# Starting the input projection inside the first norm: three weight tiles, first token group

## What is computed

```python
h = _rms(x, P['norm_mix_pre'])
proj = jnp.einsum('btd,dc->btc', h, P['w_in'])
hq, hf, hi, hg, rw, sq, sk, sv, gq, gk, gv, ga, gg = _split(proj, IN_WIDTHS)
```

## Time and profile before

| | us |
|---|---|
| median of 3 runs | 2010.35 (2009.53 to 2010.56) |
| span of the profiled execution | 2008.4 |
| TensorE busy | 1819.3 (91%) |
| VectorE busy | 821.1 (41%) |
| ScalarE busy | 614.2 (31%) |
| GpSimd busy | 396.8 (20%) |

### The profile page before, as it was taken

One profiled execution on the slowest core, in us unless ns is written; L12 is line 12 of the kernel. 1 busy time (PEld: TensorE's weight loads), 2 busy tenths in 40 slices (PEclk: granted clock), 3 DMA queues, 4 the chain that ended last, 5 costly groups with the idle time before them and its releaser, 6 DMA issues.

```text
span 2008.4 us, 33890 instructions
## 1 busy us (share of the span) xinstructions
PE 1819.3 (91%) x13839; PEld 1519.3 (76%) x13839; DVE 821.1 (41%) x1320; ACT 614.2 (31%) x1421; POOL 396.8 (20%) x606
## 2 busy tenths in 40 slices
PE   4999999999775798788887996999999999999996
PEld 4999999844454666388873445999999999999995
DVE  7111111166337764734321454344444444433336
ACT  3111111266355554523321222222222222222223
POOL 6400021288335454320010001000000000000004
PEclk9999999999887755689978997999999999999998
DMA  5211131200461111000004101111111111121102
GB/s 150 59 42 34 42 95 56 72 26 1 125 179 41 32 27 29 12 2 2 2 1 156 34 26 53 42 42 42 42 51 54 42 42 42 43 58 45 42 21 89
DMA packets 103829, 100.07 MB, mean 50 GB/s; under 512 B 15522, under 2 KB 89906, under 8 KB 103714
## 3 DMA queue, kind: packets, MB, share of 16 engines
q1 hardware_dynamic: 91266, 81.15, 13.8%
q0 software_dynamic: 6720, 17.11, 2.9%
q10 hardware_dynamic: 5728, 0.19, 0.2%
HBM read 85.78 MB, written 12.65 MB: 49 GB/s over the span
## 4 chain that ended last, share of the span: by engine, by line
PE 51%; DVE 4%; ACT 1%; DMA 1%; issue 1%; POOLq 0%; POOL 0%; SPq 0%; DVEq 0%
PE ps L416 12%; PE ps L418 12%; PE ps L417 12%; PE ps L2422 6%; PE ps L2063 1%; PE ps L2084 1%; PE ps L2080 1%; PE ps L1987 1%; DVE arena L2596 1%; DMA arena<-in_w_out 1%; PE ps L2515 1%; PE ps L2514 1%; PE ps L2136 0%; DVE arena L2173 0%; PE ps L2134 0%
## 5 line engine op out<-in xcount | busy, mean ns | idle before, releaser
L416 PE MATMUL ps<-h_split,w_split 128*128 128x384 f32 (+1 forms) x768 | 251.1, 327 | 3.4 <-DVE w_split L2577 3.4
L418 PE MATMUL ps<-h_split,w_split 128*128 128x384 f32 (+1 forms) x768 | 250.9, 327 | 0.0
L417 PE MATMUL ps<-h_split,w_split 128*128 128x384 f32 (+1 forms) x768 | 250.8, 327 | 0.0
L2607 DVE TENSOR_TENSOR arena<-arena,ps 128x1024 f32<-128x1024 f32 x144 | 175.6, 1220 | 148.7 <-PE ps L418 139.8
L418 PE MATMUL ps<-w_split,u_split 128*128 128x512 f32 x512 | 199.4, 389 | 0.0
L417 PE MATMUL ps<-w_split,u_split 128*128 128x512 f32 x512 | 199.3, 389 | 0.0
L416 PE MATMUL ps<-w_split,u_split 128*128 128x512 f32 x512 | 199.2, 389 | 0.0
L2637 POOL TENSOR_TENSOR arena<-arena 128x1024 f32<-128x1024 f32 (+1 forms) x9 | 22.3, 2482 | 760.1 <-DVE arena L2596 760.1
L2585 DVE TENSOR_TENSOR u_split<-above_u_split,u_split 128x384 fp32r<-128x384 f32 (+1 forms) x96 | 49.4, 515 | 295.9 <-ACT above_u_split L2558 295.8
L2537 ACT ACTIVATE w_split<-below_w_split 128x1024 fp32r<-128x1024 f32 x64 | 64.1, 1048 | 325.0 <-PE ps L418 307.5
L416 PEld LDWEIGHTS ps<-h_split,w_split 128*128 128x128 f32 x768 | 144.7, 188 | 4.2 <-issue 3.6
(11 more groups left out here) (389 smaller groups left out, 3622.5 us busy)
## 6 DMA issues: line engine op xcount, KB each, us to landing
below_w_split<-in_w_up SPq DMA_DIRECT2D x32, 512.0 KB, 5.0
below_w_split<-in_w_down SPq DMA_DIRECT2D x32, 512.0 KB, 4.0
w_raw<-in_w_in SPq DMA_DIRECT2D x27, 512.0 KB, 4.0
arena<-in_x_prompt SPq DMA_DIRECT2D x16, 512.0 KB, 3.7
arena<-in_cache_sb_k SPq DMA_DIRECT2D x64, 128.0 KB, 2.8
arena<-in_cache_sb_v POOLq DMA_DIRECT2D x64, 128.0 KB, 2.9
nat_scratch<-nat_stage POOLq DMA_DIRECT2D x32, 128.0 KB, 2.0
arena<-nat_scratch SPq DMA_DIRECT2D x16, 256.0 KB, 2.8
```

The source lines that it names most:

```text
L416: pe.matmul(out, w_hi, x_hi, start=first, stop=False)
L417: pe.matmul(out, w_hi, x_lo, start=False, stop=False)
L418: return pe.matmul(out, w_lo, x_hi, start=False, stop=last)
L2607: dve.tensor_tensor(y, y, p, ALU.add).then_inc(S("dn_out"), 1)
```

## The change

Nine jobs change their place. Units 0 to 2 run with token group 0 first (jobs 0 to 2), then with group 1 (3 to 5), then with group 2 (6 to 8); the 45 others keep the order of before. Jobs 0 to 2 are cut in half (12 products each) and issued inside the norm, half a job behind the transposes of each of tiles 3 to 8. In front of each of the three jobs TensorE waits for the unit's split and for `hT` 6, the first three tiles of h.

For this SP loads weight tiles 0, 1 and 2 behind tiles 2, 4 and 6, and VectorE splits them behind the scaling and the eviction in its turns 2, 4 and 6. The six banks of the projection are now 4, 5, 6, 7, 3, 0 in that order, the shift transposes go to bank 2, and jobs 4 and 5 wait until the norm has read banks 3 and 0. Job 3 waits for `hT` 12, job 6 for `hT` 18. ScalarE's wait for all of h moves behind its first six evictions. The later units' loads and splits are as before, and the slot and bank bookkeeping follows the new order.

```diff
+EARLY = 3
-    return ([(name, "T", a, tg) for name, a, _ in T_UNITS for tg in range(3)]
+    early = [T_UNITS[u][:2] + (tg,) for tg in range(3) for u in range(EARLY)]
+    late = [(name, a, tg) for name, a, _ in T_UNITS[EARLY:] for tg in range(3)]
+    return ([(name, "T", a, tg) for name, a, tg in early + late]
...
-    PBANKS = 6
+    P_BANKS = (4, 5, 6, 7, 3, 0)
+    PBANKS = len(P_BANKS)
...
                 sp.dma_start(xin[0:rows(i), i % 3, :], x_rows(i)).then_inc(S(f"x_in{i % 3}"), 16)
+                if i in (2, 4, 6):
+                    load_w_in(sp, i // 2 - 1)
...
                 if i >= 1:
                     evac(i - 1)
+                if i in (2, 4, 6):
+                    split_w_in(dve, i // 2 - 1)
...
                     ins.then_inc(S("xT"), 1)
+                if i >= 3:
+                    n, k0 = (i - 3) // 2, KD // 2 * ((i - 3) % 2)
+                    if k0 == 0:
+                        pe.wait_ge(S("w1_split"), n + 1)
+                        pe.wait_ge(S("hT"), 6)
+                    project_T(pe, n, k0, k0 + KD // 2)
 
             pe.wait_ge(S("params"), 16 * N_PAR_DMA)
+            pe.wait_ge(S("h_tmp"), 2 * NT - 3)
             for ct in range(RWT):
-                ins = pe.transpose(ps[:, 6, ct * NB:(ct + 1) * NB], shift_in[0:NB, ct * P:(ct + 1) * P],
+                ins = pe.transpose(ps[:, 2, ct * NB:(ct + 1) * NB], shift_in[0:NB, ct * P:(ct + 1) * P],
...
+        def project_T(pe, n, k0, k1):
+
+            name, _, a, tg = JOBS[n]
+            u = [unit[:2] for unit in T_UNITS].index((name, a))
+            cw, (t0, tw) = T_UNITS[u][2], EG[tg]
+            w_hi, w_lo = (w1[:, y, w_slot(u), :, 0:cw] for y in range(2))
+            for k in range(k0, k1):
+                ins = three(pe, ps[0:cw, P_BANKS[n % PBANKS], 0:tw], w_hi[:, k, :], w_lo[:, k, :],
+                            h_hi[:, k, t0:t0 + tw], h_lo[:, k, t0:t0 + tw], k == 0, k == KD - 1)
+            if k1 == KD:
+                ins.then_inc(S("proj_ps"), 1)
 
         def project_tensor(pe):
-            pe.wait_ge(S("hT"), 2 * NT)
...
+            for n in range(EARLY, NTJ):
+                name, _, a, tg = JOBS[n]
+                if n == EARLY:
+                    pe.wait_ge(S("hT"), 12)
+                if n in (4, 5):
+                    pe.wait_ge(S("h_tmp"), 2 * NT - 2 if n == 4 else 2 * NT - 1)
+                if n == 2 * EARLY:
+                    pe.wait_ge(S("hT"), 2 * NT)
+                if n >= 3 * EARLY and tg == 0:
+                    pe.wait_ge(S("w1_split"), [unit[:2] for unit in T_UNITS].index((name, a)) + 1)
+                if n >= PBANKS:
+                    pe.wait_ge(S("proj_out"), n - PBANKS + 1)
+                project_T(pe, n, 0, KD)
...
         def project_act(act):
-            act.wait_ge(S("hT"), 2 * NT)
-            act.wait_ge(S("shiftT"), 1)
             for n, (name, kind, a, tg) in enumerate(JOBS):
+                if n == 2 * EARLY:
+                    act.wait_ge(S("hT"), 2 * NT)
+                    act.wait_ge(S("shiftT"), 1)
```

More of the change, by code:

```diff
@@ L429, in w_slot_free @@
             v = before[-1]
-            return 3 * (v + 1) if v < len(T_UNITS) else NTJ + NT * ((v - len(T_UNITS)) // 2 + 2)
-        def project_sync(sp):
[L433 to L439, removed]
@@ L441, in project_tensor @@
-        def project_tensor(pe):
-            pe.wait_ge(S("hT"), 2 * NT)
[L443 to L454, removed]
+            if v >= len(T_UNITS):
+                return NTJ + NT * ((v - len(T_UNITS)) // 2 + 2)
@@ new lines, in w_slot_free, with load_w_in, split_w_in @@
+            return JOBS.index((T_UNITS[v][0], "T", T_UNITS[v][1], 2)) + 1
+        def load_w_in(sp, u):
+            name, a, cw = W_UNITS[u]
+            c0 = COL[name] + a * P
+            sp.dma_start(w1_raw[:, u % RSLOTS, 0:KD * cw].rearrange("p (k c) -> p k c", k=KD),
+                         A["w_in"][0].rearrange("(k p) c -> p k c", p=P)[:, :, c0:c0 + cw])\
+                .then_inc(S(f"w_in{u % RSLOTS}"), 16)
+        def split_w_in(dve, u):
+            name, a, cw = W_UNITS[u]
+            raw = w1_raw[:, u % RSLOTS, 0:KD * cw].rearrange("p (k c) -> p k c", k=KD)
+            w_hi, w_lo = (w1[:, y, w_slot(u), :, 0:cw] for y in range(2))
+            dve.wait_ge(S(f"w_in{u % RSLOTS}"), 16 * (u // RSLOTS + 1))
+            if w_slot_free(u):
+                dve.wait_ge(S("proj_ps"), w_slot_free(u))
+            dve.tensor_copy(w_hi, raw).then_inc(S("w1_hi"), 1)
+            dve.wait_ge(S("w1_hi"), u + 1)
+            dve.tensor_tensor(w_lo, raw, w_hi.bitcast(F32), ALU.subtract).then_inc(S("w1_split"), 1)
@@ new lines, in project_sync @@
+        def project_sync(sp):
+            for u in range(EARLY, len(W_UNITS)):
+                sp.wait_ge(S("w1_split"), u - RSLOTS + 1)
+                load_w_in(sp, u)
+        def project_T(pe, n, k0, k1):
+            name, _, a, tg = JOBS[n]
+            u = [unit[:2] for unit in T_UNITS].index((name, a))
+            cw, (t0, tw) = T_UNITS[u][2], EG[tg]
+            w_hi, w_lo = (w1[:, y, w_slot(u), :, 0:cw] for y in range(2))
+            for k in range(k0, k1):
[3 more added lines that the diff above has]
+                ins.then_inc(S("proj_ps"), 1)
@@ new lines, in project_tensor @@
+        def project_tensor(pe):
+            for n in range(EARLY, NTJ):
[11 more added lines that the diff above has]
+                project_T(pe, n, 0, KD)
+            n = NTJ
@@ L460, in project_tensor @@
                 for a in range(2):
-                    ins = pe.transpose(ps[0:r, n % PBANKS, a * P:(a + 1) * P], skT[:, a, i * P:i * P + r], ident)
+                    ins = pe.transpose(ps[0:r, P_BANKS[n % PBANKS], a * P:(a + 1) * P], skT[:, a, i * P:i * P + r], ident)
                 ins.then_inc(S("proj_ps"), 1)
@@ L470, in project_tensor @@
                     pe.wait_ge(S("proj_out"), n - PBANKS + 1)
-                    out = ps[0:r, n % PBANKS, 0:GW].rearrange("p (a c) -> p a c", a=2)
+                    out = ps[0:r, P_BANKS[n % PBANKS], 0:GW].rearrange("p (a c) -> p a c", a=2)
                     for k in range(KD):
@@ L478, in project_act @@
         def project_act(act):
-            act.wait_ge(S("hT"), 2 * NT)
-            act.wait_ge(S("shiftT"), 1)
             for n, (name, kind, a, tg) in enumerate(JOBS):
+                if n == 2 * EARLY:
+                    act.wait_ge(S("hT"), 2 * NT)
+                    act.wait_ge(S("shiftT"), 1)
                 act.wait_ge(S("proj_ps"), n + 1)
-                bank = ps[:, n % PBANKS, :]
+                bank = ps[:, P_BANKS[n % PBANKS], :]
                 if kind == "N":
@@ L517, in project_vector @@
             dve.tensor_copy(rwP[:, :, 1 + T:].rearrange("p c (b t) -> p c b t", b=NB)[:, :, :, 0],
[L518 to L528, removed]
+                            ps[:, 2, 0:RWT * NB].rearrange("p (c b) -> p c b", c=RWT)).then_inc(*did("dve"))
+            for u in range(EARLY, len(W_UNITS)):
+                split_w_in(dve, u)
         NAT_JOBS = [(name, i) for name in N_GROUPS for i in range(NT)]
```

## The result

| | before | changed |
|---|---|---|
| median, us | 2010.45 (2009.53 to 2015.75, 4 runs) | 1998.81 (1996.77 to 2000.23, 4 runs) |
| span of the profiled execution, us | 2008.4 | 1998.3 |

The ratio is 0.9938, with a 95% interval of 0.9924 to 0.9952: 11.6 us less by the medians. The forecast was 10.8 us.

What follows compares the result with a forecast made beforehand. TensorE, 91% busy, bounds the kernel, with its hole in the opening norm, paced by VectorE. Three such jobs done at 59.34 us, less 48.5 us, gives 10.8 us; 2010.35 - 10.8 = 1999.5 us, range 1996.5 to 2006.0 us.

Steps and rivals of the forecast that it cites:

- The frame held: Opening norm: VectorE sets its pace at 3.71 us a tile; three jobs, 12.48 us of TensorE at full rate, move into it.
- The gains' delay: Gains on ScalarE's queue share engines with weight 0's transfer: between no delay and 1.9 us; taken as none.
- The split: VectorE's split of a weight tile inside the norm: 2.26 us each, three times, 6.78 us ahead of tile 8's scaling.
- Rival 1: Norm: splits and GpSimd's subtractions block each other, a split takes 3.57 us; gain 6.9 us, 2003.4 us; chance 0.08.
- the forecast of 42.1 us for tile 8's scaling: VectorE's scaling of tile 8: 35.32 us in before plus 6.78 us for three splits.
- The end of the norm: After tile 8's scaling: 0.79 us to its transposes, 1.11 transposes, 2.08 last half-job, 0.91 shift transposes; X = 47.0 us.
- The clock at the end: Last half-job and job 3 onwards: low clock costs up to 4.53 us; 1.5 us taken, so X in effect 48.5 us.
- Rival 2 and 3: Norm clock: 1.2 GHz for much of it, 2005.1 us, chance 0.09; or no half-job raised, 2011.3 us, chance 0.10.
- Rival 4: First half-job waits past 26 us, half-jobs run behind the norm; at 30 us gain 7.6 us, 2002.7 us; chance 0.03.
- Downstream: Stages after the opening: later loads wait for semaphores and move along, so the gain is carried through whole.
- The new waits of jobs 4 to 6: Waits for banks 3 and 0 and hT 18: hidden behind the last half-job and jobs 3 to 5.

## Why the prediction was right, step by step

The time, 1998.8 us for 1999.5 us forecast, comes from the mechanism that was forecast. Its terms were less exact than the sum: five of them were off, by +1.0, +1.7, -1.1, -0.6 and -1.5 us of job 3's start, and they nearly cancel. That the forecast is within a microsecond is in part luck.

- **The frame held.** VectorE sets the end of the norm, and the moved products are the gain. The kernel with the products twice shows the second (12.56 us for 12.48), the one where GpSimd reads nothing the first (tile 8 7 us earlier, job 3 at 41.76 instead of 48.01 us).
- **The gains' delay was named and set at zero.** It measured 0.99 us (tile 1 scaled at 10.70 instead of 9.71 us). The reason given, that tile 0's eviction has the load of tile 1 behind it, missed the order on VectorE: the wait for the gains stands ahead of tile 1's scaling, and it is for both gains, where this norm needs the first. The bound of 1.9 us was right.
- **The split was mis-sized.** 2.26 us were taken from the row at 41.60 us; it measured 2.80, 2.83 and 2.83 us, 1.7 us in all. That row had the last, short subtraction beside it (256 columns), the splits inside the norm the full ones. Rival 1 had this mechanism, at 3.57 us a split. Here the cast began 0.16 us ahead of GpSimd's subtraction and took its 0.68 us, and only VectorE's subtraction waited (2.17 for 1.23 us). Its full price of 3.58 us appeared in the kernel with ScalarE's casts, where both instructions do.
- **A return that was not in the sum.** Behind a split the next cast of h takes 0.43 us instead of 0.79, because GpSimd has run out of work: 3 x 0.36 = 1.1 us back. With 0.99 + 1.7 - 1.1 = 1.6 us the forecast of 42.1 us for tile 8's scaling becomes 43.7; it was 43.76.
- **The end of the norm.** From tile 8's scaling to job 3 I had 0.79 + 1.11 + 2.08 + 0.91 = 4.89 us; it took 4.25 us, as transposes at full clock are shorter than the half-rate rows that I used.
- **The clock at the end.** 1.5 us were set aside for a low clock behind the norm, and nothing was paid. The rise came at 30.46 us, 4.5 us behind the first product and half a microsecond ahead of the second half-job, within which it was forecast. It then stayed, but the forecast compared it with the wrong row: 64% busy was counted for TensorE behind the rise, near the 72% of the row at 660 us with its mean of 0.76. In fact TensorE had tiles 5 and 6 waiting for it and was busy for 11.69 of 13.65 us (86%). The kernels with quarter and whole jobs show that the concern was real: with larger pauses the clock fell, at a cost of 2.9 us in the second. Together: 48.5 + 1.6 - 0.6 - 1.5 = 48.0 us, which is where job 3 starts.
- **Rival 2 and 3** (transposes hold the clock down) fall by the rise at 30.46 us, and by the quarter-jobs, where it came at 30.23 us with six products between transposes. What the Trainium skill says in TensorE: Matmul & The Clock Gate, Part 4, that the full clock does not engage for transposes, is not tested by these two kernels, which had products between the transposes; see below.
- **Rival 4** falls: the first half-job waited until 25.93 us, just inside the limit of 26 us named for it.
- **Downstream** nothing was given back up to the sk mark, and the medians differ by the same 11 to 12 us. The new waits of jobs 4 to 6 show no idle time: GpSimd's last subtraction ends at 51.4 us, job 6 starts at 60.62 us. The profiled spans differ by only 10.1 us, which is within the scatter of the later stages.

## What to carry to other kernels

Work that fills an idle engine in a stage bound by another is worth its full length behind the stage, less what its preparation costs on the engine that binds. So cost the preparation (here the splits) by rows with the same neighbours on the other engines: a row from the end of a stage, where the neighbour has run dry, is too cheap. Spread the filling over all the waits (half a job behind every tile, not a whole one behind every second), so that TensorE has no long pause. Request no large transfer beside a small one that the binding engine waits for, and let it wait only for what it needs.

## What the runs showed of the hardware that was not expected

- VectorE's operations on SBUF lengthen beside GpSimd's subtractions, and the lengthening is passed on: without the weight casts the microsecond moved from the subtraction (2.17 to 1.21 us) to the next scaling (0.74 to 1.76 us). It vanished when GpSimd only wrote. The traces show who pays: in the changed kernel each of the three casts of weights begins some 0.16 us ahead of GpSimd's subtraction and takes 0.68 us, and GpSimd's takes 1.64 to 1.67 instead of 1.26 us; with ScalarE's casts of h each begins some 0.4 us behind GpSimd's and takes 1.41 to 1.43 us. The one that begins second waits. This agrees with the exclusive port of the Trainium skill (SBUF — State Buffer, Who interferes with whom).
- Transposes alone can raise the clock. In the kernel with ScalarE's casts of h, 16 transposes ran in a row from 9.79 us, ahead of any product, and the granted clock of the stretches is:

```profile
9.79 3.36 PE L415 MATMUL ps<-arena 128*128 128x128 f32 x16 [0.34 <-DVE arena L385]
...
12.54:15.95 3.41, 0.61 (x6) 0.37 (x4) 2.58 (x3) 2.39 (x7) 3.10 (x4) 1.00 1.08 286
15.95:26.19 10.24, 4.86 (x17) 4.49 (x18) 8.41 (x10) 6.58 (x16) 6.84 (x5) 0.50 0.87 227
```

A recorded rise at 12.54 us and a fall at 15.95 us, with nothing but transposes before them; TensorE is idle from 13.15 us on. The durations agree: the 16 transposes take 3.36 us, where twice eight at half rate are 3.94 us. It is one trace. The Trainium skill's sentence that the full clock does not engage for transposes (TensorE: Matmul & The Clock Gate, Part 4) did not hold in this trace.
